# Token-shifted low-rank products, sample state products and router of a two-layer hybrid decoder step: other operand layouts

## The reference

```python
h = _rms(x, norm_mix)                                # layer 1
prev = concatenate([shift0[:, None], h[:, :-1]], 1)  # token shift; shift0: state_shift, zero for the prompt
xr, xw, xk, xv, xa, xg = [h + (prev - h) * mu[i] for i in range(6)]
r = xr @ wr; k = xk @ wk; v = xv @ wv
w_log = -softplus(-(w0 + tanh(xw @ w1) @ w2)) - 0.5  # w1: 1024 x 64, w2: 64 x 1024
a = sigmoid(a0 + (xa @ a1) @ a2)                     # a1: 1024 x 64
g = sigmoid(xg @ g1) @ g2                            # g1: 1024 x 128
# a scan over tokens per head (16 heads of 64) with the state S:
S = S * w_t + (S @ a_t) b_t^T + v_t k_t^T;  y_t = S @ r_t
# mixture of experts
logits = h2 @ router                                 # 1024 x 8
top_v, top_i = top_k(logits, 2); gates = softmax(top_v)
```

## Time and profile before

| | before |
|---|---|
| median of 3 runs | 1747.38 us |
| lowest, highest | 1741.54, 1748.83 us |
| the profiled execution | 1750.27 us |
| its span | 1748.6 us |
| its mean granted clock of TensorE | 0.967 |
| TensorE busy | 1683.8 us, 96% |
| VectorE busy | 1177.0 us, 67% |
| ScalarE busy | 918.6 us, 53% |

### The profile page before, as it was taken

The page is one execution under the profiler, slowest core; times in us unless marked ns, Lnnn a source line. Parts: engine busy times, 40 slices in busy tenths (PEclk is TensorE's granted clock), DMA queues, the critical chain, the costliest instruction groups (busy, mean ns, idle before and its releaser), DMA issues.

```text
span 1748.6 us, 25799 instructions
## 1 busy us (share of the span) xinstructions
PE 1683.8 (96%) x10101; PEld 1393.0 (80%) x10101; DVE 1177.0 (67%) x1525; ACT 918.6 (53%) x1193; POOL 148.0 (8%) x180
## 2 busy tenths in 40 slices
PE   9999699999997899999999999999999999999999
PEld 7776477999995677999867787888878787878787
DVE  5652722677657454444444788979797989888897
ACT  3442521543327243433223577767686868777774
POOL 1102100000000013322021200000000000000011
PEclk9999879999998999999797899999999999999999
DMA  8832422554322330000024989989797989899893
GB/s 349 356 133 86 199 97 103 224 194 155 145 86 97 123 118 0 2 1 2 2 103 169 393 335 380 411 326 423 313 427 312 423 355 383 356 380 392 348 421 142
DMA packets 41097, 405.03 MB, mean 232 GB/s; under 512 B 4784, under 2 KB 5072, under 8 KB 11664
## 3 DMA queue, kind: packets, MB, share of 16 engines
q1 hardware_dynamic: 34336, 372.64, 53.0%
q0 software_dynamic: 6672, 31.14, 4.4%
HBM read 379.49 MB, written 26.30 MB: 232 GB/s over the span
## 4 chain that ended last, share of the span: by engine, by line
PE 89%; DVE 7%; ACT 2%; issue 1%; DMA 1%; DVEq 0%; ACTq 0%; SPq 0%; POOL 0%; POOLq 0%
PE ps L2260 85%; DVE rest_ring L2072 1%; DMA ring<-in_moe_w 1%; PE ps L3010 1%; PE ps L2702 1%; PE ps L2650 1%; DVE ring L1553 0%; DVE arena L1522 0%; DVE arena L1648 0%; ACT arena L1151 0%; PE ps L2963 0%; DVE arena L1531 0%; PE ps L2928 0%; DVE arena L1661 0%; DVE arena L1527 0%
## 5 line engine op out<-in xcount | busy, mean ns | idle before, releaser
L2260 PE MATMUL ps<-head,hsel 128*128 128x512 f32 x1408 | 458.9, 397 | 4.5 <-DVE rest_ring L2072 4.5
L2072 DVE TENSOR_TENSOR rest_ring<-ring,head 128x2048 fp32r<-128x2048 f32 (+1 forms) x160 | 328.0, 2070 | 6.6 <-ACT head L1384 6.5
L2260 PEld LDWEIGHTS ps<-head,hsel 128*128 128x128 f32 x1408 | 265.0, 188 | 63.9 <-DVE rest_ring L2072 7.8
L2260 PE MATMUL ps<-arena,ring 128*128 128x288 f32 (+9 forms) x1552 | 276.8, 350 | 10.1 <-DVE arena L1864 6.6
L1384 ACT ACTIVATE head<-ring 128x2048 fp32r<-128x2048 f32 (+1 forms) x160 | 274.3, 1741 | 18.9 <-DMA ring<-in_moe_w 18.7
L2260 PEld LDWEIGHTS ps<-arena,ring 128*128 128x128 f32 (+4 forms) x1552 | 214.1, 200 | 69.8 <-issue 17.1
L2260 PE MATMUL ps<-rest_ring,hsel 128*128 128x512 f32 x576 | 225.0, 391 | 0.0
L2260 PE MATMUL ps<-head,actT_split 128*128 128x512 f32 x512 | 168.8, 393 | 7.4 <-issue 5.6
L2260 PE MATMUL ps<-rest_arena,head 128*128 128x288 f32 x704 | 174.7, 296 | 0.0
L2260 PE MATMUL ps<-rest_arena,rest_ring 128*128 128x288 f32 x528 | 155.5, 294 | 0.0
L2260 PE MATMUL ps<-h,ring 128*128 128x288 f32 (+2 forms) x624 | 135.2, 374 | 1.8 <-DVE h L1493 1.8
(11 more groups left out here) (364 smaller groups left out, 2402.4 us busy)
## 6 DMA issues: line engine op xcount, KB each, us to landing
ring<-in_moe_w SPq DMA_DIRECT2D x72, 2048.0 KB, 11.1
ring<-in_moe_w SPq DMA_DIRECT2D x72, 1024.0 KB, 7.5
arena<-in_moe_w SPq DMA_DIRECT2D x16, 2048.0 KB, 14.3
ring<-in_ffn_w SPq DMA_DIRECT2D x11, 2048.0 KB, 7.4
arena<-in_moe_w SPq DMA_DIRECT2D x16, 1024.0 KB
ring<-in_ffn_w SPq DMA_DIRECT2D x11, 1024.0 KB, 5.0
moe_rows<-arena POOLq DMA_DIRECT2D x1, 6656.0 KB, 33.8
ring<-in_w_in SPq DMA_DIRECT2D x2, 3072.0 KB, 13.1
```

What stands on the lines that cost most here:

```text
L2072: V.tensor_tensor(mrest[s][:, o:o + w], mslot[s][:, o:o + w], mhead[c % 2][:, o:o + w].bitcast(F32), ALU.subtract).then_inc(sem("gu_split" ...
L2260: return nc.tensor.matmul(o, l, r, start=start, stop=stop, skip_group_check=skip)
```

## The change

It alters three structures of layer 1.

**1. Hidden products of w and a.** The root `rs` is a factor per token, and the mix is linear, so the products are made from raw tiles `x * nm1` (written by ScalarE into `xi[0]` between the squares). VectorE builds weights of 128 columns per tile, `(1 - mu) W` beside `mu W` (`both_shares`, in the last feed-forward group). TensorE gets both products, 64 rows each, in one bank, and for the samples' first tokens eight more columns from `state_shift`. VectorE then multiplies by `rs`, shifts the second half by one token and adds (`joined_hidden`). `mix(0)`, `mix(1)` and their own shares disappear. Hw now stands ahead of N3 on TensorE, and Ra ahead of Hg.

**2. sZY.** `ar_both` is a moving operand in which the two heads of a tile lie in separate columns, the other head's rows zero. One product of 128 x 64 weights by 16 columns stands for two of 64 x 64 by 8.

**3. The router.** `router` is the stationary operand (8 columns), all 288 tokens are streamed; eight products. The 8 x 288 result is copied to `expert_rows` and turned to token rows by three transposes. The sum of squares of tile 6 is made a tile earlier.

The diff, cut to its core:

```diff
+        raw = xi[0]
+        prev_hid = Us[0:64, 0:T]
...
+        ar_both = AR[:, :, 1, 0:P].rearrange("p k (r a t) -> p k r a t", r=2, a=2)
...
+        expert_rows = sel_last[0:NE, :]
...
+        def both_shares(nm):
+
+            o = (where["lora"] % RING) * SLOT + 5120
+            t = ring[:, o:o + 1024] if nm == "w" else xi2[:, KT * T:KT * T + 1024]
+            return t.rearrange("p (k s n) -> p k s n", k=KT, s=2)
...
-        for name, n in (("Hw", 1), ("Ha", 1), ("Rw", 8), ("Hg", 1), ("Ra", 8), ("Rg", 8)):
+        for name, n in (("Hw", 1), ("Ha", 1), ("Rw", 8), ("Ra", 8), ("Hg", 1), ("Rg", 8)):
...
-            squares(sq3, x, lambda k: emptied(act, base[f"FD{FC - 1}"] + k), "sq_ready")
+            for k in range(KT):
+                emptied(act, base[f"FD{FC - 1}"] + k)
+                A(sq3[:, k, :], x[:, k, :], ACT.Square).then_inc(sem("sq_ready"), 1)
+                A(raw[:, k, :], x[:, k, :], ACT.Copy, scale=v("nm1", k)).then_inc(sem("h_head"), 1)
             inverse_roots([base["N3"]], [rs[0]], 1.0 / D, eps_cols[EPS], "rs_ready")
             load_functions(SIGMOID_TANH)
-            users = [base["Hw"], base["Ha"], base["Hg"], base["Rk7"]]
+            users = [base["Ha"], base["Ha"], base["Hg"], base["Rk7"]]
...
             def own_share(n):
 
                 mrow = (1, 4, 5, 2, 0, 3)[n]
-                if n >= 2:
-                    full(act, users[n - 2])
+                full(act, users[n - 2])
...
-            own_share(0)
-            own_share(1)
-            hidden("w", ACT.Tanh)
+            emptied(act, base["Hw"])
+            A(hid[0][0:64, :], hid[0][0:64, :], ACT.Tanh).then_inc(sem("hid_tanh"), 1)
             own_share(2)
-            hidden("a", ACT.Copy)
             lora_out("w", sw, "w0")
+            lora_out("a", aT, "a0")
             own_share(3)
             emptied(act, base["Rw"] + 7)
             hidden("g", ACT.Sigmoid)
-            lora_out("a", aT, "a0")
             own_share(4)
...
-                    zy = bank(g).rearrange("p (n a l) -> p n a l", a=2, l=DL)
-                    A(z1T.rearrange("p k (b l) -> p (k b) l", l=DL), zy[:, :, 0, :], ACT.Copy)
-                    A(y1.rearrange("p k (b l) -> p (k b) l", l=DL), zy[:, :, 1, :], ACT.Copy).then_inc(freesem(g), 1)
+                    zy = bank(g).rearrange("p (i b r a l) -> p i b r a l", b=DB, r=2, a=2, l=DL)
+                    for i_, dst in enumerate((z1T, y1)):
+                        for u in range(2):
+                            for r in range(2):
+                                ins = A(dst[64 * r:64 * r + 64, u:KT:2, :].rearrange("p k (b l) -> p k b l", l=DL),
+                                        zy[64 * u:64 * u + 64, :, :, r, i_, :], ACT.Copy)
+                    ins.then_inc(freesem(g), 1)
...
+                if c == FC - 1:
+                    loaded(dve, "lora")
+                    o = VEC["mu"][0]
+                    for nm, mrow, at in (("w", 1, 0), ("a", 4, 512)):
+                        for i, share in enumerate((ommu[:, 8 * mrow:8 * mrow + 8], vec[:, o + 8 * mrow:o + 8 * mrow + 8])):
+                            V.tensor_tensor(both_shares(nm)[:, :, i, :], W("lora")[:, at:at + 512].rearrange("p (k n) -> p k n", k=KT),
+                                            share.unsqueeze(2).broadcast_to([P, KT, 64]), ALU.mult).then_inc(sem("shares_ready"), 1)
...
-            norm(base["N3"], "nm1", "h_tile")
+            def joined_hidden(nm, dst):
+
+                g = base["H" + nm]
+                full(dve, g)
+                b = bank(g)
+                old = prev_hid[:, TP:T].rearrange("p (b l) -> p b l", l=DL)
+                V.tensor_tensor(prev_hid[:, 1:TP], b[64:P, 0:TP - 1], rs[0][64:P, 0:TP - 1], ALU.mult)
+                V.tensor_tensor(old[:, :, 1:DL], b[64:P, TP:T].rearrange("p (b l) -> p b l", l=DL)[:, :, 0:DL - 1],
+                                rs[0][64:P, TP:T].rearrange("p (b l) -> p b l", l=DL)[:, :, 0:DL - 1], ALU.mult)
+                V.tensor_copy(old[:, :, 0], b[64:P, T:T + DB])
+                link(V.tensor_tensor(dst[0:64, :], b[0:64, 0:T], rs[0][0:64, :], ALU.mult))
+                V.tensor_tensor(dst[0:64, 1:T], dst[0:64, 1:T], prev_hid[:, 1:T], ALU.add).then_inc(freesem(g), 1)
+                emptied(dve, g)
+
+            emptied(dve, base["N3"])
+            n_norm[0] += 1
+            dve.wait_ge(sem("rs_ready"), n_norm[0])
+            joined_hidden("w", hid[0])
+            for k in range(KT):
+                V.scalar_tensor_tensor(h[:, k, :], x[:, k, :], v("nm1", k), rs[0], ALU.mult, ALU.mult).then_inc(sem("h_tile"), 1)
+            joined_hidden("a", hid[1])
...
-            for n in range(5):
-                mix(n)
+            mix(2)
+            V.tensor_copy(shiftout[:, :, 0], h[:, :, TP - 1]).then_inc(sem("shiftout_ready"), 1)
+            V.tensor_copy(shiftout[:, :, 1:9], hs[:, :, :, 3]).then_inc(sem("shiftout_ready"), 1)
+            mix(3)
+            mix(4)
...
+                    emptied(dve, base["QY", 1, 1])
+                    for r in range(2):
+                        V.memset(ar_both[64 * r:64 * r + 64, :, 1 - r], 0.0)
+                        V.tensor_copy(ar_both[64 * r:64 * r + 64, :, r], AR[64 * r:64 * r + 64, :, :, TP:T]).then_inc(sem("ends_scaled"), 1)
...
-                if m > 1:
+                if 1 < m < KT - 1:
                     sum_squares(xi[0], 32, m - 1)
+                if m == KT - 2:
+                    sum_squares(xi[0], 32, m)
...
+            V.tensor_copy(expert_rows, bank(g)[0:NE, 0:T]).then_inc(sem("logits_kept"), 1)
+            dve.wait_ge(sem("logits_turned"), 1)
+            lv3 = bank(g)[:, T:T + 24].rearrange("p (c e) -> p c e", c=3)
...
-            summed(base["N3"], 2, sq3, C("ones"))
-            loaded(pe, "lora")
...
+            def both_hidden(nm):
+
+                g = base["H" + nm]
+                w = both_shares(nm).rearrange("p k s n -> p k (s n)")
+                b = take(g)
+                for k in range(KT):
+                    if nm == "w":
+                        pe.wait_ge(sem("h_head"), KT + k + 1)
+                    mm(b[:, 0:T], w[:, k, :], raw[:, k, :], k == 0, k == KT - 1, skip=True)
+                    ins = mm(b[:, T:T + DB], w[:, k, :], shift_now[:, k, :], False, k == KT - 1, skip=True)
+                done(ins, g)
...
+                if nm == "w":
+                    pe.wait_ge(sem("hid_tanh"), 1)
...
-            hidden(0, "w")
-            hidden(1, "a")
+            pe.wait_ge(sem("shares_ready"), 4)
+            pe.wait_ge(sem("x_half_loaded"), 32)
+            both_hidden("w")
+            summed(base["N3"], 2, sq3, C("ones"))
+            both_hidden("a")
             lora_out(0, "w")
+            lora_out(1, "a")
+            loaded(pe, "lora")
             hidden(2, "g")
-            lora_out(1, "a")
             lora_out(2, "g")
...
+                    pe.wait_ge(sem("ends_scaled"), 2)
+                    zy = b.rearrange("p (n r a l) -> p n r a l", r=2, a=2, l=DL)
                     for i in range(KT):
                         for s in range(DB):
-                            for r0 in (0, 64):
-                                ins = mm(zy[r0:r0 + 64, i * DB + s], wk[r0:r0 + 64, i, s, :],
-                                         AR[r0:r0 + 64, i, :, TP + DL * s:TP + DL * (s + 1)])
+                            r0 = 64 * (i % 2)
+                            ins = mm(zy[r0:r0 + 64, i // 2 * DB + s], wk[:, i, s, :], ar_both[:, i, :, :, DL * s:DL * (s + 1)])
                     done(ins, g)
...
-                        pe.wait_ge(sem("ends_scaled"), 3)
+                        pe.wait_ge(sem("ends_scaled"), 5)
...
-                b = bank(base["RL"])
-                if k < KT:
-                    pe.wait_ge(sem("h_tile"), 2 * KT + k + 1)
-                    for c in range(2):
-                        mm(b[:, c * NE:(c + 1) * NE], h[:, k, c * P:(c + 1) * P], r3[:, k, :], k == 0 and c == 0, k == KT - 1, skip=True)
-                if k:
-                    m_ = P if k < KT else TS
-                    o = (k - 1) * T + TP
-                    return mm(b[0:m_, 2 * NE:3 * NE], hb[:, o:o + m_], r3[:, k - 1, :], False, k == KT, skip=True)
+                pe.wait_ge(sem("h_tile"), 2 * KT + k + 1)
+                return mm(bank(base["RL"])[0:NE, 0:T], r3[:, k, :], h[:, k, :], k == 0, k == KT - 1)
...
-            logits(7)
-            done(logits(8), base["RL"])
+            done(logits(7), base["RL"])
             g = base["N4"]
             pe.wait_ge(sem("sq_summed"), 3)
             for c in range(3):
                 ins = mm(bank(g)[:, c:c + 1], xi2[:, c * P:(c + 1) * P], C("ones")[:, 0:1], c == 0, c == 2, skip=True)
             done(ins, g)
+            pe.wait_ge(sem("logits_kept"), 1)
+            for c, (t0, n) in enumerate(TOK):
+                ins = nc.tensor.transpose(bank(base["RL"])[0:n, T + NE * c:T + NE * c + NE], expert_rows[:, t0:t0 + n], C("ident")[0:NE, 0:NE])
+            ins.then_inc(sem("logits_turned"), 1)
```

(17 more changed lines are left out.)

5 lines of the change are left out of this document (1 added, 4 removed).

## The result

| | before | changed |
|---|---|---|
| median | 1748.11 us (6 runs, 1740.84 to 1751.18) | 1733.00 us (6 runs, 1729.92 to 1734.56) |
| profiled execution, its span | 1750.27, 1748.6 us | 1734.56, 1732.9 us |
| mean granted clock | 0.967 | 0.978 |
| TensorE busy | 1683.8 us | 1669.5 us |

The ratio is 0.9915, interval 0.9897 to 0.9932: 0.85% faster, 15 us. The forecast was 1740.7, 0.4% faster; 1733.0 is the very end of its range, and the gain is more than twice the 6.7 us that I said.

The account below looks back on a forecast made before the run. The prediction took TensorE to bound the kernel, at 89% of the chain. Terms of -3.0, +0.3 and -4.0 summed to -6.7 us, giving 1740.7 us from the median 1747.38, with a range of 1733 to 1748.5.

Parts of the forecast that it names:

- the rule to look for waits and clock: Whole kernel: an edit pays only where it removes TensorE work, a TensorE wait, or time at TensorE's lower clock.
- The sixteen sigmoids: Start of layer 1, ScalarE: eight of w and eight of a at 3.9 us each, helping set the pace before Rg.
- the wait before Rg: Start of layer 1: TensorE waits about 3 us for ScalarE; its absence would show the forecast wrong.
- one other wait of 1.51 us: Wait at 891.44 followed by slower records; basis for charging the new layer 1 wait 1.4 us at half speed.
- rival 2: Start of layer 1: 8-column records hide under wide ones, or the new wait costs no clock; 4 us more, chance 0.13.
- Rival 3: Start of layer 1: the clock falls inside Hw and Ha, +11.5 us, so 1752.2, slower than before; chance 0.07.
- 128 records at twice the pitch are 256 at the old: sZY: products keeping one column strip double the record pitch, so halving the products gains nothing; value +0.3 us.
- the pitch of QU: sZY pricing: 0.061 us a record where all products use the same strips, against 0.030 for QS, which alternate.
- my -2.5: sZY: lower bound of its value, for the case that the fall of the clock comes later.
- a sign of being wrong: sZY: the stage should still take 10 to 13 us; under 8 us would show the forecast wrong.
- Rival 1: sZY: records cost by number, not load; the stage falls from 12.6 to 6.3 us, whole 1734.4; chance 0.10.
- the credit of the wide streams: Router, seventh and eighth output columns: wide streams replace small products and keep the clock up, taking 1.7 us off.
- the tail: After the router, from 946.6 to 971: low clock begins later, worth between 0 and -2.8 us, -1.4 taken.

Follow-up runs that it names:

- part 1 alone: The kernel before with only the hidden products of w and a made from raw tiles and Ra ahead of Hg; 1740.54 us, ratio 0.9960.
- held: The kernel before with sZY's loop over the two heads of a tile moved outermost, 64 products in a row on the same strips; 1754.46 us, one run.
- alternating strips: The changed kernel with sZY's two loops exchanged, samples outside, so the column strip changes from product to product; 1723.75 us, ratio to before 0.9861.
- part 3 alone: The kernel before with only the router changed; 1741.46 us, ratio 0.9976.
- part 3 undone: The changed kernel with the router's old products; 1732.99 us (5 runs).
- alternating strips in the kernel before: The kernel before with only sZY changed and its loops exchanged so that the column strip changes from product to product; 1730.65 us (4 runs).
- part 2 alone: The kernel before with only sZY changed, loops as in the changed kernel; 1738.32 us, ratio 0.9944.

## Why the prediction was wrong

**What bounds the kernel: right,** and so was the rule to look for waits and clock. Parts 1 and 2 act where I put them. Of part 3, what acts in the changed kernel's profile is the clock, which part 3 isn't needed for.

**Part 1: right mechanism, -3.0 said, -6.6 measured.** Hw starts 0.13 us after its forerunner, a tile takes 0.71 us (I had 0.72), Ha is full 11.9 us after the feed-forward (12.1). The four VectorE products that build the weights cost TensorE nothing, as I had taken it. Two terms were off, 2.9 of the 3.6 us. The sixteen sigmoids take 6.33 us, where I had twice the 3.90 of the earlier trace rows: the rows' eight came every 0.49 us, the pace of TensorE's two records, and these sixteen every 0.40, so the rows' mean is no price. That makes the wait before Rg 1.23 us, not 3. And this wait did not cost any clock: 543.60 to 557.20 and what follows is at 1.00. Charging it with 1.4 us, from one other wait of 1.51 us, was wrong here. The second half of rival 2 had this, with 0.13. Rival 3, a fall of the clock inside Hw and Ha, did not come: they ran at 1.00 throughout.

**Part 2: the failing step.** I wrote that 128 records at twice the pitch are 256 at the old, nothing gained, and gave +0.3. Measured is -5.6. One half is the pitch: alone the part gains 3 us with the clock falling at the same place (9.8 against 12.8), since a quarter of the records start beside the block before. I had taken the pitch of QU, sixteen records without a change of strip, for blocks that change strips every sixteen. The other half is the clock: in the changed kernel it falls 4.6 us into the stage and not 1.3, and the stage takes 7.1 us instead of 9.8. Together that is outside my -2.5, and the stage stayed under the 8 us that I had named as a sign of being wrong. Why the clock falls later isn't shown. An earlier start alone doesn't do it: with part 1 alone the stage begins at 838.4 and the clock falls 1.6 us into it. And with the same sZY it came 4.6, 4.6 and 2.5 us in, so the same code takes 7.1 or 8.8 us: some 1.6 of the 5.6 us are chance.

Rival 1, that records cost by number, has the right sign, but number alone is the wrong reason: held and alternating strips change the time by a factor of 2 with the number of records fixed. Where the strips alternate its pitch is right, 0.029 us for the 128 records too. The Trainium skill, TensorEngine Tiling (Array Packing), Key Properties, says that different tiles load weights and multiply in parallel. These runs agree: 12.8 against 25.8 us, and at the full clock a mean of 0.029 against 0.046 us a record. The same page of the Trainium skill, under Instruction Overhead, gives about 60 cycles a product, 0.025 us at 2.4 GHz by an estimate. That is near the 0.029 us of alternating records and not the 0.058 of those on one strip.

**Part 3: -4.0 said; -12.9 up to the experts, of which 6.6 came back.** The records are as costed, 28 + 6 + 14 in 5.8 us against 10 + 2 + 4 in 4.4; but with the transposes and the waits only 0.2 us of this is left on the way to the 48 products. The clock stays at 1.00 through the seventh and eighth column, which I had put at -1.7 and to the credit of the wide streams. It comes with part 3 alone, but the old products run without the fall as well (part 3 undone, and alternating strips in the kernel before): their eight columns are no sufficient cause. RK waits 0.4 us for the choice. What I mis-sized is the tail: I let its low clock start later by up to 2.8 us and took 1.4. It went altogether. That is 5 to 6 us of time and not part 3's doing alone, since part 2 alone and even the unchanged kernel can have it.

Against the lower group, which I take for the executions with the same tail, the kernel before is at 1741, the changed one at 1733, and the 8 us are parts 1 and 2: 1741 to 1738 for part 2 alone, 5 for the lower group of part 1 alone. By the profiles with a fast tail (1741.54 and 1734.56) it is more: from the last feed-forward product on, 1213.1 and 1201.2 us, so 11.9, of which a layer 0 that was 4.9 us longer in the second hid a part. Which of the two holds on average isn't settled. The median of 1748 stood in the upper group, and so did the profile from which I worked; three runs, one of them at 1741.54, had shown both groups already, and I read the spread as noise.

**What I left out** is the end of the gain: in the first expert TensorE waits for weights behind the store of the states, and its clock falls behind the wait. These 6.6 us hid the size of part 3's error.

The sum by its own steps: -3.0 + 0.3 - 4.0 = -6.7 was said; in the profiles it is -6.6 - 5.6 - 12.9 + 6.6, and +1.6 from layer 0 and +1.2 between the parts: -15.7. Two sums of mine were wrong in themselves. The parts' own lower bounds, -8.0, -2.5 and -5.5, add to -16.0 and not to -12, which gives 1731.4: that 1733.0 fell on the very end of the range comes of this. And the chances of rivals 1 and 2 add to 0.23, not 0.21.

## What to carry to other kernels

Where small products are bound by weight loads, let neighbouring products use different strips of the array; the order of a loop alone was worth a factor of 2 here (25.8 to 12.8 us), more than halving the number of products in blocks (12.8 to 9.8). Before pricing a change, sort the times of all executions: two groups mean that one profile shows only one of two behaviours, so take a second one. And a gain ahead of a stage that streams weights ends where the first transfer waits for a buffer; follow the chain to what holds that buffer.

## What the runs showed of the hardware that I had not expected

- Sixteen records on one strip do not all wait for the block before: on a change of strip about four of the next block's sixteen ran beside the block before (a mean pitch of 0.080 us at half the clock, where two records on the same strip are 0.107 apart).
- The same program had the tail of 24 us at 0.50 in one profile and at 1.00 in another, with the same small products ahead of it. Of 40 further times 29 lie near the first and 11 near the second.
- The clock fell while TensorE was busy without a break: in the changed kernel it was at 1.00 over 841.5 to 846.1, busy 4.60 of 4.60 us with records of 16 columns, and at 0.50 from there. With alternating strips the same products ran at 1.00 to their end.
- In the profile of the changed kernel a wait of TensorE of 1.23 us (before 557.22) left the clock at 1.00; behind one of 1.51 us (before 880.45) the granted clock was 0.51 to 883.70.
